# Moving the output projection of a hybrid decoder layer inside its last pair of heads

## The reference: what is computed

```
h = rmsnorm(x, attn_norm_w);  p = h @ w_in                       # 512 tokens x 1024
o_da = differential attention, 4 heads of 128
o_rw = RWKV-7 time mixing, 8 heads of 64
x = x + concat(o_da, o_rw) @ w_out                               # "x2"; w_out is 1024 x 1024
h = rmsnorm(x, ffn_norm_w)
logits = h @ router_w + router_b;  the 4 best of 32 experts per token, softmax gates
x = x + sum over the 4 experts of gate * (clamped SwiGLU(h @ mlp1_w[e] + mlp1_b[e]) @ mlp2_w[e] + mlp2_b[e])
return rmsnorm(x, final_norm_w)
```

## Time and profile before

| what | value |
|---|---|
| median of 3 runs | 1547.91 us (1543.93 to 1552.13) |
| profiled execution, its own time | 1548.19 us |
| span of its core | 1546.5 us |
| busy share of the span | PE 94%, DVE 79%, ACT 66%, POOL 30% |
| first piece of the projection starts | 375.31 us |
| mask of choices | 435.44 us |
| first expert's rows reach TensorE | 446.05 us |

### The profile page before, as it was taken

The page is one execution under the profiler, slowest core; times in us unless marked ns, Lnnn a source line. Parts: engine busy times, 40 slices in busy tenths (PEclk is TensorE's granted clock), DMA queues, the critical chain, the costliest instruction groups (busy, mean ns, idle before and its releaser), DMA issues.

```text
span 1546.5 us, 25543 instructions
## 1 busy us (share of the span) xinstructions
PE 1450.2 (94%) x9333; PEld 1071.9 (69%) x9334; DVE 1227.3 (79%) x1068; ACT 1013.2 (66%) x997; POOL 458.8 (30%) x253
## 2 busy tenths in 40 slices
PE   6999999996989999999999999999999999999884
PEld 5677777775867686777767677776777767656553
DVE  5565656565469799998989899889988989888984
ACT  4635353525256577776877878777777877677773
POOL 7200000000018431544425355322634525222210
PEclk9999999997979999999999999999999999999997
DMA  6211111004469899999999999999999999999992
GB/s 206 62 46 52 43 38 50 26 16 162 156 257 382 312 400 398 413 404 403 383 397 410 395 402 408 399 373 389 401 401 399 409 393 408 371 391 393 399 394 92
DMA packets 96941, 457.47 MB, mean 296 GB/s; under 512 B 11198, under 2 KB 37998, under 8 KB 47584
## 3 DMA queue, kind: packets, MB, share of 16 engines
q1 hardware_dynamic: 86176, 429.63, 69.5%
q0 software_dynamic: 10688, 26.80, 6.3%
HBM read 443.57 MB, written 18.10 MB: 299 GB/s over the span
## 4 chain that ended last, share of the span: by engine, by line
PE 38%; DMA 12%; DVE 10%; issue 9%; ACT 4%; POOL 2%; SPq 1%; DVEq 0%; ACTq 0%; POOLq 0%
DMA w_pieces<-in_mlp_w 10%; PE psum L2179 8%; PE psum L2200 5%; DVE w_pieces_lo L1943 5%; PE psum L2182 5%; PE psum L2250 4%; PE psum L2255 3%; PE psum L1387 3%; PE psum L2192 3%; PE psum L2189 3%; ACT w_pieces_hi L1743 3%; POOL slot_lists L1685 2%; DVE av L1968 1%; PE psum L2223 1%; DVE silu L1956 1%
## 5 line engine op out<-in xcount | busy, mean ns | idle before, releaser
L1943 DVE TENSOR_TENSOR w_pieces_lo<-w_pieces,w_pieces_hi 128x2048 fp32r<-128x2048 f32 x346 | 781.6, 2284 | 105.9 <-ACT w_pieces_hi L1743 104.3
L1743 ACT ACTIVATE w_pieces_hi<-w_pieces 128x2048 fp32r<-128x2048 f32 x346 | 660.8, 1915 | 245.7 <-DMA w_pieces<-in_mlp_w 174.4
L1676 POOL DMA_INDIRECT sum_rows<-ys,this_i x30 | 270.2, 9008 | 339.4 <-ACT ys L1795 196.6
L2250 PE MATMUL psum<-w_pieces_hi,ah 128*128 128x512 f32 x512 | 147.6, 392 | 7.0 <-DVE ah L1952 6.6
L2255 PE MATMUL psum<-w_pieces_lo,ah 128*128 128x512 f32 x512 | 139.9, 395 | 14.9 <-DVE w_pieces_lo L1943 14.8
L2200 PE MATMUL psum<-w_pieces,x_native 128*64 128x512 f32 x288 | 131.3, 598 | 0.0
L2189 PE MATMUL psum<-w_pieces_hi,xh 128*128 128x512 f32 x432 | 125.7, 414 | 2.9 <-ACT w_pieces_hi L1743 2.9
L2192 PE MATMUL psum<-w_pieces_lo,xh 128*128 128x512 f32 x432 | 119.3, 398 | 8.1 <-DVE w_pieces_lo L1943 8.1
L2255 PEld LDWEIGHTS psum<-w_pieces_lo,ah 128*128 128x128 f32 x512 | 95.3, 189 | 41.4 <-DVE w_pieces_lo L1943 22.4
L2179 PE MATMUL psum<-w_pieces_hi,xh 128*128 128x512 f32 x440 | 123.7, 403 | 0.0
L2182 PE MATMUL psum<-w_pieces_lo,xh 128*128 128x512 f32 x440 | 119.0, 392 | 1.1 <-DVE w_pieces_lo L1943 0.2
(11 more groups left out here) (421 smaller groups left out, 2233.3 us busy)
## 6 DMA issues: line engine op xcount, KB each, us to landing
w_pieces<-in_mlp_w SPq DMA_DIRECT2D x384, 1024.0 KB, 9.3
w_raw<-in_w_in SPq DMA_DIRECT2D x26, 512.0 KB, 4.0
w_pieces<-in_w_out SPq DMA_DIRECT2D x8, 512.0 KB, 9.3
chunk_work<-in_x SPq DMA_DIRECT2D x4, 512.0 KB, 6.6
sc<-pall POOLq DMA_DIRECT2D x16, 128.0 KB, 4.0
x<-in_x SPq DMA_DIRECT2D x4, 512.0 KB, 13.8
sum_rows<-x POOLq DMA_DIRECT2D x4, 512.0 KB, 3.2
h_rows<-w_pieces POOLq DMA_DIRECT2D x4, 512.0 KB, 2.9
```

Source lines behind the costliest of these rows:

```text
L1676: nc.gpsimd.indirect_dma_start(sum_dram, bass.IndirectOffsetOnAxis(this_i[rows, 0:1], 0), ys[rows, :], None, bounds_check=S - 1, oob_is_er ...
L1743: nc.scalar.activation(hi[:, p % RING], raw[:, raw_slot(b, p)].rearrange("p r n -> p (r n)"), ACT.Copy).then_inc(s_hi, done)
L1943: nc.vector.tensor_tensor(lo[:, p % RING], raw[:, raw_slot(b, p)].rearrange("p r n -> p (r n)"), hi[:, p % RING].bitcast(F32), ALU.subtrac ...
L2250: nc.tensor.matmul(bank(into + c), a[:, 2 * p + r2, :], hi[:, p % RING, r2 * D + c * 512:r2 * D + (c + 1) * 512], start=p == 0 and r2 == 0 ...
```

## The change

The output projection is moved from the second part into the last pair of the first part. In the last pair, `fold(count)` stands where `fill` stood in the earlier ones, and multiplies the six blocks of `o_t` of earlier pairs; after the pair the rest follows. `w_out` is split in buffers of `front` whose content is done with, and x is loaded again there. x2, its squares and roots are complete when the block ends. The second part turns, routes and normalises all four row tiles at once. SP's guards on the first six pieces are gone, since their buffer is no longer shared. The biases lie in the lo ring, and their low parts are made behind the sort of the experts.

```diff
+OUT_ORDER = (0, 4, 1, 5, 2, 6, 3, 7)
+READY = 6
+FOLD_ORDER = (4, 5, 6, 7, 0, 1, 2, 3)
+FINAL_BANKS = (4, 5, 2, 3, 6, 7, 0, 1)
...
     @block.sync
+        for i, k in enumerate(OUT_ORDER):
+            if i < 2:
+                sp.wait_ge(s_wlo, IN_TILES + i - 1)
+            else:
+                sp.wait_ge(s_wout_lo[i - 2], 1)
+            sp.dma_start(w_out_raw(i), w_out_v[:, k, :]).then_inc(s_w[i % 2], 16)
+            if i == 2:
+                sp.wait_ge(PE.sem, PE.reached(HEADS - 1, "v_turn"))
+                sp.wait_ge(DV.sem, DV.reached(HEADS - 1, "ks"))
+                for t in (2, 3, 0, 1):
+                    sp.dma_start(x[:, t, :], x_v[:, t, :]).then_inc(s_xr, 16)
...
     @block.gpsimd
+        pool.wait_ge(s_emptied, 16)
+        for i in range(4):
+            lower_o(i)
+            if i == 1:
+                lower_w_out(1)
+        lower_w_out(3)
+        for i in range(4, READY):
+            lower_o(i)
+        lower_w_out(5)
+        lower_o(READY)
...
     @block.scalar
+                split_out(0)
+                raise_o(0)
+                raise_o(1)
+                split_out(1)
+                raise_o(2)
+                raise_o(3)
             copy_out(n0 + 2)
             exponents(0)
...
+                split_out(3)
             exponents(1)
...
+        raise_o(7)
+        for t in range(NT):
+            if t >= 2:
+                act.wait_ge(s_ss, t - 1)
+            act.wait_ge(s_x2, t + 1)
+            nc.scalar.activation(flat(w_raw[:, t % 2]), x[:, t, :], ACT.Square, accum_out=stat[:, 24 + t:25 + t]).then_inc(s_ss, 1)
+        act.wait_ge(s_ss, NT)
+        nc.scalar.activation(stat[:, 28:32], stat[:, 24:28], ACT.Sqrt, bias=con("eps"), scale=1.0 / D).then_inc(s_root, 1)
...
     @block.vector
+        def add_part(f):
+            t, c = divmod(FOLD_ORDER[f], 2)
+            dve.wait_ge(s_folded, f + 1)
+            dve.wait_ge(s_xr, 16 * NT)
+            part = x[:, t, c * 512:(c + 1) * 512]
+            nc.vector.tensor_tensor(part, bank(4 + f % 2), part, ALU.add).then_inc(s_fold, 1)
...
     @block.tensor
+        def project_out(u, i, o, first, last):
+            t, c = divmod(u, 2)
+            for m, (a, w) in enumerate(((o_hi[i], w_out_part(i, False)), (o_hi[i], w_out_part(i, True)), (o_lo(i), w_out_part(i, False)))):
+                ins = nc.tensor.matmul(o, a[:, t * P:(t + 1) * P], w[:, c * 512:(c + 1) * 512], start=first and m == 0, stop=last and m == 2)
+            return ins
...
+        folds = iter([(f, i) for i in range(READY) for f in range(2)] + [(f, i) for f in range(2, KT) for i in range(READY)])
...
             output(0)
             fill(n0 + 3, 0, 2)
+            fold(4)
...
     def route_sync(sp):
-        for k in range(KT):
-            sp.dma_start(wo[:, k, :], w_v[:, k, :]).then_inc(s_w[k], 16)
-        for t in range(NT):
-            sp.dma_start(x[:, t, :], d["x"][0, t * P:(t + 1) * P, :]).then_inc(s_xr, 16)
...
-        sp.wait_ge(s_bias, 3)
         for p in range(RAW):
-            if p == 1:
-                sp.wait_ge(s_store, 16 * NT)
-                sp.wait_ge(s_log, NT)
-            if p == 3:
-                sp.wait_ge(g["s_gath"], 16)
             sp.dma_start(raw[:, p].rearrange("p r n -> p (r n)"), gate_up_rows(d, 0, p)).then_inc(g["s_raw"][p], 16)
...
     def route_gpsimd(pool):
         for t in range(NT):
             nc.gpsimd.dma_start(g["sum_dram"][t * P:(t + 1) * P, :], x[:, t, :]).then_inc(g["s_kept"], 16)
+        for t in range(NT):
             pool.wait_ge(s_h2, t + 1)
             nc.gpsimd.dma_start(g["h2_dram"][t * P:(t + 1) * P, :], h2[:, t, :]).then_inc(s_store, 16)
+        pool.wait_ge(s_log, NT)
+        g["zero_rows"]()
         pool.wait_ge(s_store, 16 * NT)
...
     def route_vector(dve):
+        chain(nc.vector.reciprocal(stat[:, 32:36], stat[:, 28:32]))
+        copied(1)
         dve.wait_ge(s_fw, 16)
+        normed(0)
+        copied(3)
...
+        dve.wait_ge(s_bh, 1)
+        for rows in (slice(32, 64), slice(96, 128)):
+            nc.vector.tensor_tensor(bias[rows, :], bias_raw[rows, :], bias[rows, :].bitcast(F32), ALU.subtract).then_inc(s_bias, 1)
...
     def up(r, b, act):
...
+                pe.wait_ge(g["s_bias"], 3)
```

More of the change, by code:

```diff
@@ L150, in sb, with two_views @@
             return stack.enter_context(nc.sbuf_tensor(name, shape, dt))
+        def two_views(name, stack, shape):
+            with ExitStack() as gone:
+                rounded = sb(gone, name + "_rounded", shape, F32R)
+            return sb(stack, name, shape), rounded
         def sem(name):
@@ L318, in tile_of, with flat, w_out_raw, w_out_part @@
         return pall[:, group, shift:shift + S]
+    def flat(a):
+        return a.rearrange("p a b -> p (a b)")
+    def w_out_raw(i):
+        return flat(w_raw[:, (IN_TILES + i) % 2])
+    def w_out_part(i, low):
+        if i < 3:
+            return flat((w_lo if low else w_hi)[:, (IN_TILES + i) % 3])
+        if i < READY:
+            return flat((h_lo if low else h_hi)[:, 2 * (i - 3):2 * (i - 3) + 2, :])
+        at = 4 * (i - READY) + 2 * low
+        return flat(shared_r[:, at:at + 2, :])
+    o_hi = [lora_r[:, n, :] for n in range(4)] + [a[:, KT - 2 + n, :] for a in (h_hi, h_lo) for n in range(2)]
+    def o_lo(i):
+        return g["o_low"][:, OUT_ORDER[i], :]
     def less(j, n):
@@ L515, in _ @@
                 split(n0 + 4)
+            else:
+                split_out(2)
             weights_turned(0)
@@ L524, in _ @@
             output_copied(1)
+            if not more:
+                raise_o(4)
+                raise_o(5)
+                split_out(4)
             exponents(2)
@@ L532, in _ @@
                 split(n0 + 6)
+            else:
+                split_out(5)
             act.wait_ge(PE.sem, PE.reached(j, "akv"))
@@ L552, in _ @@
                 split(n0 + 7)
+            else:
+                split_out(6)
             act.wait_ge(DV.sem, DV.reached(j, "shade"))
@@ L558, in _ @@
                 copy_out(n0 + 5)
+            else:
+                split_out(7)
+                raise_o(6)
             act.wait_ge(PE.sem, PE.reached(j, "y_sum"))
@@ L763, in _ @@
             weights(3)
+            if not more:
+                add_part(0)
+                add_part(1)
             dve.wait_ge(PE.sem, PE.reached(j, "chunk"))
@@ L783, in _ @@
                 split(n0 + 7)
+            else:
+                split_out(6)
+                add_part(2)
+                add_part(3)
             dve.wait_ge(PE.sem, PE.reached(j, "o_turn"))
@@ L833, in fill, with fold @@
                     tile(n, a, b)
+            def fold(count):
+                if not more:
+                    for _ in range(count):
+                        fold_step(*next(folds))
             def dv(name):
@@ L1041, in _ @@
             y_within(4)
+            fold(1)
             state(4)
@@ L1074, in output_and_route @@
 def output_and_route(nc, d, sb, sem, st, g, con, ident, psum, bank):
-    x, stat, o_t, rank, info, flags, raw, bias = (g[k] for k in ("x", "stat", "o_t", "rank", "info", "flags", "raw", "bias"))
+    x, stat, o_t, rank, info, flags, raw, bias, rows, rwf, rb = (g[k] for k in ("x", "stat", "o_t", "rank", "info", "flags", "raw", "bias", "bias_rows", "rwf", "rb"))
     rank_at, expert_at, pick_at = g["rank_at"], g["expert_at"], g["pick_at"]
     down_b, gates_t = g["down_b"], g["turned"]
-    s_w = [sem(f"w_out_loaded{k}") for k in range(KT)]
```

301 lines of the change are left out of this document (147 added, 154 removed).

## The result

The changed kernel is slower: 1570.74 us (median of 4 runs, 1567.56 to 1573.38) against 1549.72 us of the kernel before in the same set (4 runs), ratio 1.014 with a 95% interval of 1.0104 to 1.0176. The forecast was 1548 us, 1538 to 1557 with its range. The profiled execution has a span of 1571.6 us, that of the kernel before 1546.5. A difference of 1 to 3 us between two traces, counted from the start, is therefore not yet an effect; times counted from the mask repeat far better.

The account below looks back on a forecast made before the run. The expert stream, at DMA share 1.0 and about 400 GB/s from 550 us, was taken as the bound, its start set by the slot lists. First rows +1.6 and lists -1.5 gave +0.1 on 1548.2: 1548 us, range 1538 to 1557.

Parts of the forecast that it names:

- Multiplying: Output projection's 192 matmuls, 43.5 us, begun inside the last pair and filling 5.3 of idle: last product at 403.6.
- new waits in the pair: Last pair: ScalarE's wait for w_out(3), 2 us, and GpSimd's subtractions slowing VectorE, 1 us; last product at 406.6.
- The locking by GpSimd: Last pair: ten GpSimd subtractions slow VectorE instructions beside them; bounds 0 and 11 us, taken as 1.
- the slower rival: Last pair, between scores and z7: GpSimd's subtractions lock VectorE, costing 8 to 10 us, 1557 us; chance 0.15.
- The wait for `w_out(3)`: Last pair: block queued behind x loads delays ScalarE's exponents, so PE waits 2 us, bounds 0 and 5.
- To the mask: Second part's start at B = 411.1 to the mask: 17.0 us, mask at 428.1, 7.3 earlier than before.
- To the first rows: Gather waits for h2 stores slowed by the pieces; first rows at B + 36.5 = 447.6, 1.6 later than before.
- the stores' share: After B, h2 stores on GpSimd's queue get about a third of the DMA rate beside the pieces, ending near B + 31.
- Bias subtractions hidden: Three VectorE instructions, 3.7 us, between sort and first expert's splits: hidden by the late gather, taken as 0.
- The lists: Slot lists on GpSimd, 55.8 us before: fewer loads in flight shorten them by 1.5 us, bounds 0 and -4.
- The end moves by what the lists move, and by nothing else: Expert stage: all six slots are full during the slot-list stall, so prefetched pieces give nothing and the stream is untouched.

Follow-up runs that it names:

- the version with the three edits: Changed kernel with both waits before the first pieces restored, GpSimd's subtractions held until k is rotated, x loads behind w_out(3): 1551.7 us, 1.0036; with spacer 1545.0 us, 0.9985.

## Why the prediction was wrong, by its own steps

The sum said +0.1 and +21.0 came. Of the 20.9 between them, 8.5 lie in the start of the second part, 5.0 between it and the first rows, 2.3 in the lists and 5.1 behind the lists. The first three are terms of the sum that were sized too small; the last had no term at all.

**Multiplying and the new waits in the pair: both found, both sized too small.** I had the second part beginning at B = 411.1; it began at 419.6. With the two causes removed it began at 411.5. The locking by GpSimd was put at 1 us and gave back 5.6 when removed, 4.9 of them behind the point where the edit acts; it is the slower rival's mechanism, below its price of 8 to 10. I argued that VectorE idles in the pair, but the first five subtractions fall where it doesn't, on the three instructions in a row that can be locked out. The wait for `w_out(3)` was put at 2 and gave back 3.1, of which 1.35 is scatter of the trace; together the two gave 8.1. Those are 8.1 us of B where I had 3; another 3.4 of the sum's optimism stand in both versions and were not looked into further (0.8 of it is there at 310 us already). Counted from 310 us, six traces of the unedited pair reach the second part over a range of 3.2 us, six with both causes removed within 0.1, so the price of the two differs from execution to execution.

**To the mask**: 18.2 instead of 17.0, since the norm row took 7.2 to land instead of 6.

**To the first rows**: PE turned them at B + 41.5, not B + 36.5. The mechanism was right: without the guards the stores are held up by the pieces, and the first rows wait for the stores. Mis-sized was the stores' share: the last one landed at 453.55, B + 34 instead of B + 31, and the gather, beside the rest of the pieces, took 6.4 instead of 5.4. The sum had 37.4 by its own terms and took 36.5. Together with B this is 15.1 against the predicted 1.6. The guards alone gave 11.6 back at the first product, 10.4 of them behind the mask.

**Bias subtractions hidden**: right, the lo part of x waited for the rows.

**The lists**: -1.5 was predicted, +0.8 came. That prefetched pieces are worth nothing when the rows are late was right: with all six ahead the second gather's indices came 7.0 us behind the first product, with three in hand (before) 6.7. The reverse I had not asked: with guards and early rows the products wait for pieces, and 2.9 of the gain are given back (9.6 against 6.7).

**"The end moves by what the lists move, and by nothing else"** is the step that failed in kind. The lists moved by 15.9 and the median by 21.0. I wrote that the change doesn't touch the stream, as the expert stage's instructions are the same. But their buffers moved, and 64 bytes of spacer alone give back 0.45% (1.014 to 1.0095), some 7 us, give or take 6; in the version with the three edits they give back 0.51%.

**The account of the loss.** One at a time the four causes give back 12, 6, 6 and 7 us in the medians, more than the 24 that they give together (1.014 to 0.9985). The traces say 11.6, 5.6 and 3.1 at the first product for the first three, of which 17.3 reach the lists, and about 6 for the address. With all four removed the change is worth nothing that can be told: against the trace of the kernel before, the mask comes 6.4 us earlier (429.0), the first product 4.4 (444.6) and the lists 1.4 to 2.6. Against the three other traces of its code it is 3.3 to 4.3, 1.3 to 2.0 and nothing that is clear of scatter; each stretch behind the mask takes a part of the gain back. The forecast of a gain near nothing was thus right for another kernel than the one that was run, and that is luck: the sum came to it with terms that were too small. Of the rivals, the slower one named the right place and the right sign, 1557; the removed guards and the address made it 1571.

## What to carry to other kernels

A guard that looks like a wait too many may be what keeps a latency-bound chain (store, gather, first product) clear of bulk loads: before taking it away, add up the bytes that can be in flight ahead of the chain's last store, and ask who needs them and when. When a change moves buffers, compare the start addresses of those that the largest stream is loaded into before and after; nothing in the diff and no wait in the profile names it. Work put on GpSimd beside VectorE cost nothing here next to VectorE instructions with an input in PSUM, and up to 2.2 us next to one with both in SBUF; list what runs there at that moment, not VectorE's busy share. And before a difference between two traces is called an effect, look at where they already differ ahead of the edit.

## What the runs showed of the hardware

Loads of 8 KB rows into a buffer 64 bytes off a multiple of 256 cost 0.2 to 0.5% of the kernel, in five pairs. The stores of h2, 512 KB each from GpSimd's queue, needed a median of 2.9 us in the kernel before; behind the four stores of x2 they needed 15.3 beside six loads of 1 MB on the other queue, 10.2 beside three and 6.0 with one ahead, and 9.4 beside six without the stores of x2. The last one before the gather took 15.6, 8.5 and 4.2, and 10.7. Three VectorE instructions of 128x512 with two SBUF inputs took 1.84, 2.88 and 1.75 us beside GpSimd's subtractions instead of 0.74, 0.68 and 0.69, those with an input in PSUM 0.64 in either case.
